# Doubling steps of a triangular inverse on strips of columns in a gated DeltaNet scan

## The reference, cut to what matters

```python
a_mat = bb[..., :, None] * kk * jnp.where(strict, decay, 0.0)
rhs = bb[..., None] * (vb - jnp.exp(gcum)[..., None] * jnp.einsum('bhcd,bhdv->bhcv', kb, S))
u = lax.linalg.triangular_solve(eye + a_mat, rhs, left_side=True, lower=True, unit_diagonal=True)
qk = jnp.einsum('bhid,bhjd->bhij', qb, kb) * decay
o = jnp.exp(gcum)[..., None] * jnp.einsum('bhcd,bhdv->bhcv', qb, S) + jnp.einsum('bhij,bhjv->bhiv', qk, u)
S_new = jnp.exp(glast)[..., None, None] * S + jnp.einsum(
    'bhcd,bhcv->bhdv', kb * jnp.exp(glast[..., None] - gcum)[..., None], u)
```

## Time and profile before

| | before |
|---|---|
| median of 3 runs | 2243.04 us (2238.78 to 2253.71) |
| the profiled execution | 2238.33 us |
| its span, first to last instruction | 2236.5 us |
| mean granted TensorE clock | 0.966 |

### The profile page before, as it was taken

The page is one execution under the profiler, slowest core; times in us unless marked ns, Lnnn a source line. Parts: engine busy times, 40 slices in busy tenths (PEclk is TensorE's granted clock), DMA queues, the critical chain, the costliest instruction groups (busy, mean ns, idle before and its releaser), DMA issues. The chain is left out here.

```text
span 2236.5 us, 25198 instructions
## 1 busy us (share of the span) xinstructions
PE 2082.5 (93%) x9079; PEld 1258.4 (56%) x9079; DVE 1408.0 (63%) x2471; ACT 688.1 (31%) x1756; POOL 520.2 (23%) x546
## 2 busy tenths in 40 slices
PE   6999999999989889989899999999989889999998
PEld 5554543444445565655443556666543687777774
DVE  2488987599978878938858422222332576666662
ACT  3445642121223433321101222221111544443441
POOL 2111200000000000001110567777301513322320
PEclk9999999999999999989999999999999899999999
DMA  4024312101123212021211344444638162232210
GB/s 129 15 78 151 114 57 96 36 24 47 47 101 144 85 39 85 19 73 43 76 52 57 106 140 138 138 139 142 215 132 296 57 195 65 66 89 74 74 46 29
DMA packets 157891, 207.33 MB, mean 93 GB/s; under 512 B 43808, under 2 KB 107608, under 8 KB 157720
## 3 DMA queue, kind: packets, MB, share of 16 engines
q1 hardware_dynamic: 134936, 152.87, 21.2%
q0 software_dynamic: 16896, 50.35, 7.4%
q10 hardware_dynamic: 5936, 2.49, 0.4%
HBM read 161.94 MB, written 43.74 MB: 92 GB/s over the span
## 5 line engine op out<-in xcount | busy, mean ns | idle before, releaser
L1737 PE MATMUL acc_ch<-xnT,w_ch 128*128 128x512 f32 x736 | 346.9, 619 | 7.3 <-ACT x_pad L1771 7.3
L1737 PEld LDWEIGHTS acc_ch<-xnT,w_ch 128*128 128x128 f32 x736 | 138.7, 197 | 158.2 <-issue 151.2
L793 PE MATMUL acc<-w_qg,xnT 128*128 128x512 f32 (+1 forms) x432 | 191.9, 598 | 5.4 <-DVE sgate L915 5.4
L1627 POOL DMA_INDIRECT kg<-in_cache_k,rowidx x128 | 132.2, 1033 | 138.6 <-DVE rowidx L1895 79.1
L952 DVE MAX8 top_v<-scores 128x8 f32<-128x4100 f32 x32 | 141.7, 4427 | 0.5
L954 DVE FIND_INDEX8 top_i<-top_v,scores 128x8 uint32<-128x4100 f32 x32 | 141.5, 4423 | 0.0
L956 DVE MATCH_REPLACE8 scores<-top_v,scores 128x4100 f32<-128x4100 f32 x32 | 141.2, 4413 | 0.0
L1634 POOL DMA_INDIRECT home<-in_cache_v,rowidx x128 | 129.3, 1010 | 39.0 <-issue 33.8
L793 PEld LDWEIGHTS acc<-w_qg,xnT 128*128 128x128 f32 (+1 forms) x432 | 78.0, 185 | 103.6 <-issue 97.7
L2697 PE MATMUL PB<-home,ogT_dn 128*128 128x512 f32 x288 | 129.2, 603 | 4.7 <-DVE rhs L2970 3.9
L793 PE MATMUL acc<-w_kvq,xnT 128*128 128x512 f32 (+1 forms) x288 | 127.4, 600 | 3.5 <-PEq L545 3.5
(11 more groups left out here) (423 smaller groups left out, 3924.8 us busy)
## 6 DMA issues: line engine op xcount, KB each, us to landing
home<-in_dn_w_in SPq DMA_DIRECT2D x7, 2048.0 KB, 8.5
w_ch<-in_dn_w_in SPq DMA_DIRECT2D x24, 512.0 KB, 4.9
qkv_d<-y_ch SPq DMA_DIRECT2D x24, 512.0 KB, 6.2
qkv_t<-qkv_d SPq DMA_DIRECT2D x8, 1536.0 KB, 8.0
x<-in_x_all SPq DMA_DIRECT2D x9, 512.0 KB, 3.9
out_y_all<-y_t SPq DMA_DIRECT2D x9, 512.0 KB, 2.7
w_z_s<-in_dn_w_in SPq DMA_DIRECT2D x1, 4160.0 KB, 13.7
w_kvq<-in_att_w_in SPq DMA_DIRECT2D x2, 2048.0 KB, 10.9
```

The source lines that it names most:

```text
L793: ins = pe.matmul(acc[rows(n), k % ACC, :], xnT[:, kk, cols(n)], w[:, kk, :], start=(kk == 0), stop=(kk == KT - 1))
L1627: pool.indirect_dma_start(kg[:, j % KR, :], None, ck, bass.IndirectOffsetOnAxis(ap=rowidx[:, u % 2, t * QT + u // 2:t * QT + u // 2 + 1], ...
L1737: ins = pe.matmul(acc[:, s, :], w[:, c % WR, k, :], xT[:, k, s * 512:(s + 1) * 512], start=(k == 0), stop=(k == KT - 1))
```

## The change

For chunks 1 to 8, steps 4 and 5, the products and subtractions take only the strips that the correction fills. dTT (both steps) is computed and subtracted on the 64 columns of the odd strips. dT of step 4 takes the 64 columns of the even strips. dT of step 5 takes only what the last step reads, rows 0 to 63 by columns 0 to 31, with 64 weight columns. Y is computed and copied in odd strips from chunk 2 on; in chunk 1 it is computed and copied in full, which writes the zeros into the even strips that stay there.

For this the middle products get homes of their own: that of step 4 lies in `kdm[0]` (k_masked, free after chunk 0), that of step 5 in Y, and that of step 6 in `Yq`, a quarter of the L buffer of step 4 that holds nothing then.

```diff
+        def strips(n, l):
+            return n >= 1 and l in (4, 5)
+
+        def strip(t, l, s):
+            return t.rearrange("p (b s c) -> p b s c", s=2, c=1 << l)[:, :, s, :]
+
+        def all_strips(t, l, s):
+            return t.rearrange("p h (b s c) -> p (h b) s c", s=2, c=1 << l)[:, :, s, :]
+
+        def mid(l):
+            return kdm[0] if l == 4 else Y
+        Yq = L[0:64, 1, :, 64:]
...
-                            ins = pe.matmul(a4(("Y", n, l, r))[:, h, :], L[:, lnum(n, l) % 2, hh, :], TT[:, p, hh, :], start=True, stop=True)
+                            dst, src = a4(("Y", n, l, r))[:, h, :], TT[:, p, hh, :]
+                            if strips(n, l) and n >= 2:
+                                dst, src = strip(dst, l, 1), strip(src, l, 1)
+                            ins = pe.matmul(dst, L[:, lnum(n, l) % 2, hh, :], src, start=True, stop=True)
...
-                            ins = pe.matmul(a4(("dTT", n, l, r))[:, h, :], T[:, hh, :], Y[:, hh, :], start=True, stop=True)
+                            dst, src = a4(("dTT", n, l, r))[:, h, :], mid(l)[:, hh, :]
+                            if strips(n, l):
+                                dst, src = strip(dst, l, 1), strip(src, l, 1)
+                            ins = pe.matmul(dst, T[:, hh, :], src, start=True, stop=True)
...
-                            ins = pe.matmul(a4(("dT", n, l, r))[:, h, :], Y[:, hh, :], T[:, hh, :], start=True, stop=True)
+                            dst = a4(("dT", n, l, r))[:, h, :]
+                            if l == 5:
+                                ins = pe.matmul(dst[0:64, 0:32], Y[:, hh, 0:64], T[:, hh, 0:32], start=True, stop=True)
+                            elif l == 4:
+                                ins = pe.matmul(strip(dst, l, 0), mid(l)[:, hh, :], strip(T[:, hh, :], l, 0), start=True, stop=True)
+                            else:
+                                ins = pe.matmul(dst, Y[:, hh, :], T[:, hh, :], start=True, stop=True)
...
-                        act.copy(Y[0:64, hs(r), 64:], a4(("Y", n, l, r))[0:64, :, 64:]).then_inc(a_act, 1)
+                        act.copy(Yq[:, hs(r), :], a4(("Y", n, l, r))[0:64, :, 64:]).then_inc(a_act, 1)
+                    elif strips(n, l) and n >= 2:
+                        act.copy(all_strips(mid(l)[:, hs(r), :], l, 1), all_strips(a4(("Y", n, l, r)), l, 1)).then_inc(a_act, 1)
                     else:
-                        act.copy(Y[:, hs(r), :], a4(("Y", n, l, r))).then_inc(a_act, 1)
+                        act.copy(mid(l)[:, hs(r), :], a4(("Y", n, l, r))).then_inc(a_act, 1)
...
-                        dve.tensor_tensor(TT[:, p, hs(r), :], TT[:, p, hs(r), :], a4(("dTT", n, l, r)), ALU.subtract).then_inc(a_dve, 1)
+                        old, new = TT[:, p, hs(r), :], a4(("dTT", n, l, r))
+                        if strips(n, l):
+                            old, new = all_strips(old, l, 1), all_strips(new, l, 1)
+                        dve.tensor_tensor(old, old, new, ALU.subtract).then_inc(a_dve, 1)
                     if l < last(n):
                         dve.wait_ge(fa, ra.filled(("dT", n, l, r)))
-                        dve.tensor_tensor(T[:, hs(r), :], T[:, hs(r), :], a4(("dT", n, l, r)), ALU.subtract).then_inc(a_dve, 1)
+                        old, new = T[:, hs(r), :], a4(("dT", n, l, r))
+                        if l == 5:
+                            old, new = old[0:64, :, 0:32], new[0:64, :, 0:32]
+                        elif l == 4:
+                            old, new = all_strips(old, l, 0), all_strips(new, l, 0)
+                        dve.tensor_tensor(old, old, new, ALU.subtract).then_inc(a_dve, 1)
```

More of the change, by code:

```diff
@@ L2608, in level @@
                         if by_blocks(n, l):
-                            ins = pe.matmul(a4(("dTT", n, l, r))[0:64, h, 64:], T[0:64, hh, 0:64], Y[0:64, hh, 64:], start=True, stop=True)
+                            ins = pe.matmul(a4(("dTT", n, l, r))[0:64, h, 64:], T[0:64, hh, 0:64], Yq[:, hh, :], start=True, stop=True)
                         else:
-                            ins = pe.matmul(a4(("dTT", n, l, r))[:, h, :], T[:, hh, :], Y[:, hh, :], start=True, stop=True)
+                            dst, src = a4(("dTT", n, l, r))[:, h, :], mid(l)[:, hh, :]
+                            if strips(n, l):
+                                dst, src = strip(dst, l, 1), strip(src, l, 1)
+                            ins = pe.matmul(dst, T[:, hh, :], src, start=True, stop=True)
                     ins.then_inc(fa, 1)
```

## The result

The changed kernel is slower: 2268.6 us median against 2242.3 before, 15 runs each, ratio 1.0095 with a 95% interval of 1.0069 to 1.0121 (the two medians alone give 1.0117). The forecast was 2239, in a range of 2229 to 2250. The profiled execution took 2269.35 us, its span is 2267.5. The runs lie between 2246 and 2273, further apart than before (2235 to 2254); a fifteenth run, 2281 us, counts as slow and is not in the ratio.

A forecast was written before the change was run, and what follows sets the result against it. It took the scan to be bound by TensorE's queue, worked off in program order with few holes. A 7.4 us gain less 3.3 for two clock falls gave 4.1 off the 2243.0 median: 2239 us, range 2229 to 2250.

The forecast's parts named there:

- Columns and weight loads: TensorE in the scan: 80 pairs a chunk with halved moving columns stay at 0.112 us each, gain 0.
- dT of step 32 to 64 and its holes: TensorE: 16 pairs from 0.112 to 0.058, 0.86 us a chunk, less 0.30 for holes at shape changes, leaving 0.56.
- The gain behind it: Second output transposes: the gated output ends earlier, the 0.37 us hole closes, 0.92 us a chunk, 7.4 over 8 chunks.
- The price of a fall: TensorE's clock in the scan: each fall costs 1.6 us, from four matmuls taking 3.61 us low, 1.98 high.
- The number of falls: TensorE's clock in the scan: two falls, between none and eight, 3.3 us in all.
- The rival that came true: Level steps: the clock falls in every chunk, 13.0 us lost against 7.4 gained, 2248.6; chance 0.16.
- the first rival: Scan: no fall of TensorE's clock, the whole 7.4 us gained, 2235.6; chance 0.28.
- The range: Whole kernel: 2229 (new holes at lower bound, level of runs) to 2250 (slower by falls, one us more).

The follow-up runs named there:

- e9: Kernel before, with VectorE's spread of T written four times instead of once, a longer hole ahead of the first dTT; ratio 1.0196 to the kernel before.
- e10: Changed kernel with VectorE's spread of T written four times instead of once; ratio 1.0451 to the kernel before.
- e5: Changed kernel with strips on TensorE in step 16 to 32 only, step 32 to 64 in full columns; ratio 1.0101 to the kernel before.
- e3: Changed kernel with dT of step 32 to 64 in full, 128 weight and 128 moving columns; ratio 1.0101 to the kernel before.
- e7: Changed kernel with VectorE's spread of T put ahead of the state update in chunks 2 to 8; ratio 0.9951 to the kernel before.
- e8: e2 with VectorE's spread of T put ahead of the state update; ratio 0.9946 to the kernel before.
- e11: e8 plus a product of 512 moving columns in the hole ahead of gc; ratio 0.9935, 2224.1 us against 2240.5 for the kernel before.
- e12: e7 plus a product of 512 moving columns in the hole ahead of gc; ratio 0.9948 to the kernel before.
- e2: Changed kernel, but on TensorE only dT of step 32 to 64 is cut, the other products in full columns; ratio 0.9982 to the kernel before.
- e1: Changed kernel with all TensorE products in full columns, narrower copies, subtractions and new homes kept; ratio 0.9977 to the kernel before.
- e4: Changed kernel plus a product of 512 moving columns per chunk in the hole ahead of step 16 to 32's first dTT; ratio 0.9965 to the kernel before.

## Why the prediction was wrong, by its own steps

**Columns and weight loads: right.** 80 pairs with 64 moving columns stayed at 0.11 us. The section of the Trainium skill that the prediction set against this ("TensorE: Matmul & The Clock Gate", section "Back-to-back issue gap") gives its shrinking gap for a matmul by itself; for a stream of load and matmul pairs it says that both set the spacing, and these rows agree with that.

**dT of step 32 to 64 and its holes: right.** 0.058 a pair; holes of 0.15 and 0.12 where I had 0.11 and 0.14; 0.59 us a chunk where I had 0.56.

**The gain behind it: right.** The hole at the second transposes closed, and an undisturbed chunk takes 48.08 us against 49.0: 0.91 where I had 0.92. The strips took VectorE 0.42 us as taken, the 64 by 128 one 0.28 instead of 0.25. Nothing took the gain back elsewhere in the chunk.

**The price of a fall: wrong, and this decided it.** The prediction took 1.6 us from four decay products at the two clock levels. That is what TensorE loses when wide products follow and the clock is back after 3.4 us, and to the chunk it is even less, 0.8 us, since a wait of 0.6 us takes up most of the rest. In the level steps a fall meets the very work that the change had thinned. The clock stayed low for 20.5 us, and that cost 8.4. e9 and e10 show it with the same hole in both kernels, 2.1 against 9.9 us a chunk. Chunk 1 shows it with the same work ahead, 3.4 against 10.2 us low. And e5, e3 and the change itself stand in order, 6.8, 13.7 and 20.5 us low, as the narrow products behind the start grow in number.

**The number of falls: too low as well.** I took two of eight; the profiled execution had four long and two short ones in seven chunks. Four at 1.6 would have been 6.5 us and the forecast 2242, inside the range; two at 8.4 would have been 2252. Between the profiled executions lie 31.0 us; the four long falls cost 33.8, and the gain takes part of that back. That makes the price the larger fault.

**The rival that came true** was the second, with the right sign and mechanism, but at a price of 1.6. At 8.4 a fall it decides not from the fifth but from the first on, 8.4 against 7.4. Beside the first rival stood the Trainium skill, same page, section "HAM oscillation — how this bites in real kernels", which ties falls to gaps in which TensorE waits for data. Here the hole was 0.9 us in both kernels, and only the one with strips around it had long falls at this place. With a hole of 4.5 us (e9) full columns had falls there too. So the hole counts together with what lies around it.

**The range** had both ends of the number of falls (none, eight) but no end for the price: it rested on one row, taken where wide products follow. No fall in the trace of before was followed by strips. But there are longer ones in it, as at the start of the scan, where the clock stayed low up to 1756.7 with TensorE busy, on products of 8 to 512 moving columns. This window, of which the last 3.3 us are at the high clock, shows it:

```profile
1747.00:1760.00 13.00, 12.58 (x61) 10.44 (x61) 7.37 (x17) 9.31 (x26) 9.42 (x13) 0.63 0.01 3
```

That a fall can last so long should have widened the range instead of leaving 1.6 alone in it.

What stays open: why one chunk has a fall and the next, alike, has none. It may depend on where the chunk lies in time (e7's falls stand in step with its chunks, e9's alternate, and the runs lie far apart), but no run tests that. Open as well is why the hole ahead of gc, which six chunks of before passed without a fall, has one in six of six chunks of e7 and five of six of e8, though e8 has nearly full columns; e11 and e12 show only that filling it ends them.

## What to carry to other kernels

Halving the moving columns of products with 128 weight columns saved nothing in this stream of alternating weights, and beside a hole it cost the clock. Cut weight columns instead (e2), or leave TensorE full and narrow only the other engines' operations (e1). Before thinning TensorE's work, look for holes beside it, and price a fall of the clock by the work that follows it, not by a fall elsewhere. A product into a bank that the next one overwrites, placed in a hole that is there anyway, cost nothing here and held the clock (e4, 48.08 us a chunk); taking the hole away instead was better still (e7, 47.87, and 47.09 with the second hole filled too, e12).

## What the runs showed of the hardware

- The granted clock stayed at 0.50 for 13.7 us while TensorE was busy 13.70 of 13.70 us and its weight loads 13.69 (e3), and it fell behind 3.40 us in which they were busy 3.40 and 3.39. Neither busy share shows that the clock is in danger.
- A change of weight shape cost a hole of 0.12 to 0.15 us behind 32 and 64 moving columns, 0.20 behind 128.
- VectorE subtracted strips of 16 or 32 columns, read from PSUM, in 421 ns for 256 elements; pieces of 64 columns on 64 partitions (the last step) took 404.
- VectorE's spread of T took 2.56 us in e7, 1.22 before. In e7 an operation of GpSimd ran beside it (the gate triangle, 1.89 us from 2092.24); before, that one had ended (1925.61) when the spread began. That the one slows the other is not shown; the runs show them side by side.

```profile
2092.66 2.56 DVE L2480 TENSOR_TENSOR T<-blk_packed,b 128x1024 f32<-128x1024 f32 x1
```
